# Loading the w3 matrices of the experts through the pool engine's DMA queue

## The chip, the cores and the metric

The kernel runs on one core of one Trainium2 chip, in float32. The metric is device time in microseconds (us). Three runs of the kernel before gave 3997.15 us as their median, from 3993.39 to 4002.57 us.

## The reference

Two transformer blocks run over 512 tokens of width 1024. The first has windowed attention beside retention, then a mixture of 64 experts; the second has two layers of latent attention, pooling and an mLSTM, each followed by a gated feed-forward part. The change touches the mixture of experts alone:

```python
def expert_block(args):
    xb, e = args
    hid = jax.nn.silu(xb @ w1[e]) * (xb @ w3[e])
    return hid @ w2[e]
```

`w1[e]` and `w3[e]` are 1024 x 512, `w2[e]` is 512 x 1024, each 2 MiB (2.10 MB) in float32. Each token is sent to two of 64 experts, with a weight for each, and the weighted results are summed.

## The kernel before

The kernel is written in blocks that follow one another; in each, every engine has its own list of instructions, and the lists meet only in semaphores. `moe_block` runs every expert with room for 32 token slots (`CAP`), so it loads all 64 experts' weights: 192 matrices, 403 MB. Experts that get more than 32 tokens would be run again in a further loop (`ov_...`).

The loop has 16 turns (`NIT`), each of two pairs (`pr`), each of two experts (`e2`). There are six weight buffers of 2 MiB: 0 and 2 hold w1 of the pair's experts, 1 and 3 hold w3, 4 and 5 hold w2. No buffer is double, so a matrix of the next pair can be loaded only when TensorE has done with the one before it.

- SyncE (SP) does the loading. For each pair it waits on `up_done` (L1120), issues w1 and w3 of both experts (L1123, L1124: w1, w3, w1, w3), waits on `down_done` (L1126) and issues both w2 (L1129). All go into one queue, in this order.
- TensorE (PE) waits until all four up matrices of the pair are there (L1162), runs 64 matmuls with them (L1169) and raises `up_done`. ScalarE and VectorE form silu times gate (L1238, L1290), TensorE turns the result (L1175), waits for the two w2 and multiplies with them (L1185), and raises `down_done`. After the second pair of a turn it gathers the next 128 token slots (L1151).
- VectorE copies the pair's result out of PSUM (L1294), and ScalarE stores it with a DMA of 256 KB in a queue of its own (L1243).
- GpSimd (POOL) has no work in this block. In the block before, it fills a part of `y_slots` with zeros by one DMA of 4 MiB (L982: 2048 rows of 2 KB). In the block after, it gathers the results by 16 indirect DMAs, each of 128 rows of 2 KB (L1324).

A row of w1 or w3 is 2 KB, of w2 4 KB; `up_src` and `down_src` put row k\*128+p on partition p, so that rows next to each other in a partition do not touch in memory.

Of the kernel before, what the change touches and what calls it, by code (L numbers as in the profile page):

```python
# [1094 lines left out]
def moe_block(nc, m, G, banks, A, y_slots):  # L1095
    w1, w3, w2 = A["moe_w1"][0], A["moe_w3"][0], A["moe_w2"][0]
    NIT = NE // 4
# [3 lines left out]
    def up_dst(slot):  # L1101
        return m.w[slot].rearrange("p (k n) -> p k n", k=KT)

    def down_dst(slot):
        return m.w[slot].rearrange("p (k n) -> p k n", k=FF // P)

    def up_src(w, e):
        return w[bass.ds(e, 1), :, :].rearrange("a (k p) n -> p (a k) n", p=P)

    def down_src(e):  # L1110
        return w2[bass.ds(e, 1), :, :].rearrange("a (k p) n -> p (a k) n", p=P)

    with nc.Block() as block:

        @block.sync
        def _(sp):
            with sp.Fori(0, NIT) as i:
                for pr in range(2):

                    sp.wait_ge(G["up_done"], 2 * i + pr + 1)  # L1120
                    for e2 in range(2):
                        e = 4 * i + 2 * pr + e2
                        sp.dma_start(up_dst(2 * e2), up_src(w1, e)).then_inc(G[f"e_in{2 * e2}"], 16)  # L1123
                        sp.dma_start(up_dst(2 * e2 + 1), up_src(w3, e)).then_inc(G[f"e_in{2 * e2 + 1}"], 16)  # L1124

                    sp.wait_ge(G["down_done"], 2 * i + pr + 1)  # L1126
                    for e2 in range(2):
                        e = 4 * i + 2 * pr + e2
                        sp.dma_start(down_dst(4 + e2), down_src(e)).then_inc(G[f"e_in{4 + e2}"], 16)  # L1129

            n = sp.value_load(m.misc_i[0:1, 1:2], min_val=0, max_val=MORE - 1)
            with sp.If(n > 0):
                sp.wait_ge(G["up_done"], 2 * NIT + 1)
                sp.wait_ge(G["down_done"], 2 * NIT + 1)
                with sp.Fori(0, n) as j:
                    e = sp.value_load(m.eb_i[0:1, bass.ds(j, 1)], min_val=0, max_val=NE - 1)
                    sp.wait_ge(G["ov_down"], j + 1)
                    sp.dma_start(up_dst(0), up_src(w1, e)).then_inc(G["ov_in"], 16)
                    sp.dma_start(up_dst(1), up_src(w3, e)).then_inc(G["ov_in"], 16)
                    sp.dma_start(down_dst(4), down_src(e)).then_inc(G["ov_in"], 16)  # L1140

        @block.tensor
        def _(pe):
# [1008 lines left out]
def program(nc, A, outs, stop=None, start=0):  # L2152
    ctx = ExitStack()
    with ctx:
# [19 lines left out]
        if start <= 1:  # L2174
            own = take(nc, G, ROUTER_SEMS + MOE_SEMS + COMB_SEMS)
            m = moe_memory(arena)
            norm_views(m, m.norm_at)
            if start == 1:
                load_x(nc, m, G, A)
            eb_dram = nc.dram_tensor("further_experts", (1, MORE), i32, kind="Internal").ap()  # L2180
            y_slots = nc.dram_tensor("y_slots", ((MAIN + MORE) * 2 * CAP, 512), f32, kind="Internal").ap()
            norm_block(nc, m, G, banks, 1 - start, "rms", m.hn, A["norm_moe_w"][0])
            router_block(nc, m, G, banks, A, eb_dram, y_slots)
            moe_block(nc, m, G, banks, A, y_slots)
            combine_block(nc, m, G, banks, y_slots)
            if stop == "moe":
                return dbg(nc, G, outs, m.h)
            give_back(nc, G, own)
# [132 lines left out]
```

## Time and profile before

| | |
|---|---|
| median of three runs | 3997.15 us |
| profiled execution, span from its first to its last instruction | 4010.2 us |
| TensorE busy | 3094.7 us (77%) |
| DMA over the span | 587 MB, mean 146 GB/s |
| loads of the experts' matrices | 192 of 2048 KB, median 19.3 us from issue to landing |

The trace gives the profiled execution no time of its own beside its span. It is one execution, and lies 13 us (0.3%) above the median of the runs. The page cuts the span into 40 slices of 100 us; a digit is a busy share in tenths. A line of a group tells the busy time, the mean of one instruction, the engine's idle time just ahead of it and what ended that.

### The profile page before, as it was taken

The page shows a single profiled execution, that of the slowest core. Times are in us where ns is not written, and L with a number is a line of the kernel's source. Part 1 is how long each engine was busy: PE and PEld are TensorE (multiplying, and loading weights), DVE is VectorE, ACT ScalarE, POOL GpSimd, SP SyncE. Part 2 cuts the span into 40 slices and gives each one's busy share as a digit, 9 for nine tenths or more (in the row PEclk, how much of TensorE's full clock was granted, in tenths as well). Part 3 has the DMA queues.
Part 4 walks back from the last instruction along what each step waited for, and adds up shares of the span by engine and source line. Part 5 has one row for each costly group of instructions (what it writes and reads, how often), then busy time and mean ns, then how long its engine had stood idle before and what let it go on. Part 6 is the DMA issues. An engine that isn't in the chain of part 4 may idle for free. (4 is left out here: it accounts for less than half of the span.)

```text
span 4010.2 us, 30222 instructions
## 1 busy us (share of the span) xinstructions
PE 3094.7 (77%) x12308; PEld 1620.9 (40%) x12308; DVE 684.3 (17%) x1670; ACT 492.8 (12%) x969; POOL 271.5 (7%) x302
## 2 busy tenths in 40 slices
PE   7999999998344545545454288879999798799997
PEld 4666666546311212112121154434444454344443
DVE  1222222101300000000000212321110223221202
ACT  1222232110100000000000112200000112010000
POOL 1000013200000000000000210010000100100001
PEclk9999999999577778777777688789999897899998
DMA  4111111121399999999999431012211210212211
GB/s 140 48 48 32 48 37 48 57 80 53 116 348 363 366 354 357 354 363 370 357 353 360 167 97 43 21 53 84 79 68 53 86 44 22 73 49 77 84 64 41
DMA packets 332165, 587.02 MB, mean 146 GB/s; under 512 B 16802, under 2 KB 143010, under 8 KB 331810
## 3 DMA queue, kind: packets, MB, share of 16 engines
q1 hardware_dynamic: 325138, 568.88, 40.0%
q0 software_dynamic: 2320, 8.39, 0.6%
q10 hardware_dynamic: 4608, 8.39, 0.5%
q8 instruction: 67, 1.10, 0.1%
q14 instruction: 32, 0.26, 0.0%
HBM read 570.96 MB, written 14.68 MB: 146 GB/s over the span
## 5 line engine op out<-in xcount | busy, mean ns | idle before, releaser
L1169 PE MATMUL bank<-arena 128*32 128x512 f32 x2048 | 297.8, 746 | 508.9 <-DMA arena<-in_moe_w 508.9
L2081 PE MATMUL bank<-arena 128*128 128x512 f32 x1408 | 608.9, 595 | 1.9 <-PEq L688 1.9
L328 PE MATMUL bank<-arena 128*128 128x384 f32 x1280 | 432.0, 490 | 14.5 <-DMA arena<-in_w_in 14.5
L2081 PEld LDWEIGHTS bank<-arena 128*128 128x128 f32 x1408 | 269.0, 191 | 340.9 <-issue 340.9
L1169 PEld LDWEIGHTS bank<-arena 128*32 128x32 f32 x2048 | 81.8, 134 | 713.4 <-issue 713.4
L328 PEld LDWEIGHTS bank<-arena 128*128 128x128 f32 x1280 | 237.9, 191 | 176.0 <-DMA arena<-in_w_in 14.8
L2093 PE MATMUL bank<-arena 128*128 128x512 f32 x704 | 302.5, 592 | 0.0
L1583 PE MATMUL bank<-arena 128*128 128x512 f32 (+3 forms) x736 | 251.0, 503 | 15.1 <-DMA arena<-in_w_in 15.1
L2093 PEld LDWEIGHTS bank<-arena 128*128 128x128 f32 x704 | 133.8, 190 | 168.4 <-issue 168.4
L1583 PEld LDWEIGHTS bank<-arena 128*128 128x128 f32 x736 | 140.9, 193 | 121.5 <-issue 74.6
L772 PE MATMUL bank<-arena 128*128 128x128 f32 x256 | 56.9, 404 | 167.4 <-POOL arena L731 105.4
L1290 DVE TENSOR_TENSOR arena<-bank,arena 64x512 f32<-64x512 f32 x32 | 22.2, 695 | 781.9 <-ACT arena L1238 781.9
L1185 PE MATMUL bank<-arena 128*32 128x512 f32 x1024 | 140.0, 696 | 15.5 <-ACT arena L1240 14.7
L1151 PE MATMUL bank<-arena 128*128 128x128 f32 x1088 | 127.4, 278 | 25.3 <-DVE arena L1280 25.3
L1151 PEld LDWEIGHTS bank<-arena 128*128 128x128 f32 x1088 | 124.2, 193 | 38.9 <-DVE arena L1280 25.5
L1238 ACT ACTIVATE arena<-bank 64x512 f32<-64x512 f32 x32 | 18.9, 590 | 851.9 <-PE bank L1169 851.9
L772 PEld LDWEIGHTS bank<-arena 128*128 128x128 f32 x256 | 48.0, 214 | 177.8 <-POOL arena L731 114.9
L2036 PE MATMUL bank<-arena 128*128 128x512 f32 x256 | 116.2, 618 | 1.8 <-PEq L1538 1.8
L325 PE MATMUL bank<-arena 128*128 128x512 f32 x256 | 110.9, 593 | 0.0
L2132 DVE TENSOR_SCALAR arena<-arena 128x512 f32<-128x512 f32 x44 | 24.0, 546 | 494.3 <-ACT arena L2108 494.3
L707 ACT ACTIVATE arena<-bank 128x512 f32<-128x512 f32 x64 | 37.4, 597 | 557.0 <-PE bank L772 557.0
L1324 POOL DMA_INDIRECT arena<-y_slots,arena x16 | 17.6, 1099 | 1226.9 <-PEq L1318 1222.4
(291 smaller groups left out, 2724.3 us busy)
## 6 DMA issues: line engine op xcount, KB each, us to landing
arena<-in_moe_w SPq DMA_DIRECT2D x192, 2048.0 KB, 19.3
arena<-in_w_up SPq DMA_DIRECT2D x44, 1024.0 KB, 7.1
arena<-in_w_in SPq DMA_DIRECT2D x52, 512.0 KB, 5.6
arena<-in_w_down SPq DMA_DIRECT2D x10, 2048.0 KB, 7.7
arena<-in_w_in SPq DMA_DIRECT2D x12, 1024.0 KB, 5.2
y_slots<-arena ACTq DMA_DIRECT2D x32, 256.0 KB, 6.5
arena<-in_w_in SPq DMA_DIRECT2D x4, 2048.0 KB, 11.3
arena<-in_w_out SPq DMA_DIRECT2D x4, 2048.0 KB, 7.8
```

What stands on the lines that cost most here:

```text
L325: ins = pe.matmul(banks[s % 2][:, :], w[:, k, tile(b)], m.aT[:, k, :], start=(k == 0), stop=(k == KT - 1))
L328: ins = pe.matmul(banks[s % 2][:, 0:CW], m.aT[:, k, tile(t)], w[:, k, :], start=(k == 0), stop=(k == KT - 1))
L707: act.activation(m.aT[:, 4 * (i % 2):4 * (i % 2) + 4, tile(i // 2)], banks[i % 4][:, :].rearrange("p (a c) -> p a c", a=4), ACT.Copy)\
L772: ins = pe.transpose(banks[i % 4][:, tile(j)], dst[:, t, tile(4 * (i % 2) + j)], m.ident)
L1151: ins = pe.matmul(banks[5 + d // 4][:, tile(d % 4)], m.hn[:, t, tile(d)], m.G[:, t, :], start=(t == 0), stop=(t == T - 1))
L1169: ins = pe.matmul(banks[pr][q:q + CAP, :], m.xt[:, k, c:c + CAP], up_dst(2 * e2 + up)[:, k, :], start=(k == 0), stop=(k == KT - 1))
L1185: ins = pe.matmul(banks[3 + pr][q:q + CAP, :], m.ht[:, f, CAP * e2:CAP * e2 + CAP], down_dst(4 + e2)[:, f, 512 * half:512 * half + 512], s ...
L1583: ins = pe.matmul(out, a, b, start=(i == 0), stop=(i == len(terms) - 1))
L2036: ins = pe.matmul(banks[n][:, :], m.mixT[:, k, tile(t)], slot_view(m, half)[:, k, :], start=(k == 0), stop=(k == KT - 1))
L2081: ins = pe.matmul(banks[2 * (j % 2) + half][:, :], w[:, k, c0:c0 + P], m.aT[:, k, :], start=(k == 0), stop=(k == KT - 1))
L2093: ins = pe.matmul(banks[2 * t + half][:, :], m.hidT[:, k, tile(t)], v[:, k % 4, 512 * half:512 * half + 512], start=(k == 0), stop=(k == N ...
L2132: own.do(dve.tensor_scalar(gc, gp[:, 0:S], m.wf[:, j, 0:1], m.wf[:, j, 3:4], ALU.mult, ALU.add))
```

## The change

SyncE no longer issues the two w3 loads of a pair. GpSimd gets a loop of its own over the same pairs: it waits on the same `up_done` and issues the two w3 loads into its own queue. Buffers, semaphores, the waits of TensorE and the further loop `ov_...` stay.

```diff
@@ moe_block, block.sync
                     for e2 in range(2):
                         e = 4 * i + 2 * pr + e2
                         sp.dma_start(up_dst(2 * e2), up_src(w1, e)).then_inc(G[f"e_in{2 * e2}"], 16)
-                        sp.dma_start(up_dst(2 * e2 + 1), up_src(w3, e)).then_inc(G[f"e_in{2 * e2 + 1}"], 16)
@@ moe_block, after block.sync
+        @block.gpsimd
+        def _(pool):
+            with pool.Fori(0, NIT) as i:
+                for pr in range(2):
+
+                    pool.wait_ge(G["up_done"], 2 * i + pr + 1)
+                    for e2 in range(2):
+                        e = 4 * i + 2 * pr + e2
+                        pool.dma_start(up_dst(2 * e2 + 1), up_src(w3, e)).then_inc(G[f"e_in{2 * e2 + 1}"], 16)
```

## Rows read from the trace of the kernel before

**Rows 1.** The page, sections 1 and 2: the span, DMA busy share in 40 slices.

```profile
span 4010.2 us, 30222 instructions
...
DMA  4111111121399999999999431012211210212211
```

**Rows 2.** The page, section 5, the costliest group: busy, mean ns, idle before.

```profile
L1169 PE MATMUL bank<-arena 128*32 128x512 f32 x2048 | 297.8, 746 | 508.9 <-DMA arena<-in_moe_w 508.9
```

**Rows 3.** Waits from 1100 to 2100 us: us in total, times, longest.

```profile
PE bank L1169 <- DMA arena<-in_moe_w: 446.4, 28, 20.5
...
PE bank L1185 <- DMA arena<-in_moe_w: 0.7, 1, 0.7
```

**Rows 4.** Windows, the expert loop: length; engines' busy us; PEclk, DMA share, GB/s.

```profile
1083.00:2240.00 1157.00, 583.79 (x4279) 252.63 (x4280) 81.02 (x131) 71.47 (x113) 0.00 (x0) 0.75 0.96 355
```

**Rows 5.** Timeline of one pair: start us, us, engine, line.

```profile
1407.28 0.37 SPq L1123 DMA_DIRECT2D arena<-in_moe_w  x1
...
1408.47 3.94 SPq L1123 DMA_DIRECT2D arena<-in_moe_w  x1
...
1409.64 5.34 PE L1185 MATMUL bank<-arena 128*32 128x512 f32 x32 [0.47 <-ACT arena L1240]
...
1412.51 6.38 SPq L1124 DMA_DIRECT2D arena<-in_moe_w  x1
...
1418.98 7.71 SPq L1129 DMA_DIRECT2D arena<-in_moe_w  x2
...
1433.34 8.88 PE L1169 MATMUL bank<-arena 128*32 128x512 f32 x64 [18.36 <-DMA arena<-in_moe_w]
...
1442.29 0.59 ACT L1238 ACTIVATE arena<-bank 64x512 f32<-64x512 f32 x1 [32.70 <-PE bank L1169]
1442.43 0.37 SPq L1123 DMA_DIRECT2D arena<-in_moe_w  x1
```

**Rows 6.** Windows, the moment after w2 has landed and before the next loads flow.

```profile
1443.00:1444.00 1.00, 0.34 (x3) 0.34 (x4) 0.60 (x1) 0.00 (x0) 0.00 (x0) 1.00 0.58 45
```

**Rows 7.** Windows, first and second 12 us of the up loads, two pairs.

```profile
1409.00:1421.00 12.00, 5.50 (x34) 1.26 (x32) 0.69 (x1) 0.39 (x1) 0.00 (x0) 0.81 1.01 349
1421.00:1433.00 12.00, 0.00 (x0) 0.00 (x0) 0.00 (x0) 0.00 (x0) 0.00 (x0) 0.50 1.05 392
...
1480.00:1492.00 12.00, 5.97 (x36) 1.58 (x36) 0.88 (x2) 0.39 (x1) 0.00 (x0) 0.84 0.98 340
1492.00:1504.00 12.00, 0.00 (x0) 0.00 (x0) 0.00 (x0) 0.00 (x0) 0.00 (x0) 0.50 1.05 394
```

**Rows 8.** Windows, the last 8 us of a pair's loads (w2).

```profile
1434.00:1442.00 8.00, 8.00 (x64) 2.23 (x56) 0.00 (x0) 0.00 (x0) 0.00 (x0) 0.81 1.02 409
```

**Rows 9.** DMA queues, 1410 to 1420 us: packets, MB, share of 16 engines' time.

```profile
q1 hardware_dynamic: 1718, 3.48, 101.3%
```

**Rows 10.** DMA queues, 1434 to 1441 us.

```profile
q1 hardware_dynamic: 713, 2.85, 102.0%
```

**Rows 11.** Line L1123, 1080 to 2200 us: issue to landing.

```profile
L1123 SPq DMA_DIRECT2D arena<-in_moe_w x64: 372/1838/4157, 1084.0 to 2194.5; - x64
...
DMA to landing us min/median/max: 8.4/13.8/20.9
```

**Rows 12.** Timeline and DMA issues: the zero fill, KB, us to landing.

```profile
1020.07 1.43 POOL L982 DMA_DIRECT2D y_slots<-arena  x1 [0.32 <-POOL arena L980]
...
y_slots<-arena POOLq DMA_DIRECT2D x1, 4096.0 KB, 14.7
```

**Rows 13.** DMA queues, 1025 to 1028 us (zero fill beside SP's small loads).

```profile
q0 software_dynamic: 276, 1.13, 91.4%
q1 hardware_dynamic: 247, 0.11, 12.8%
```

**Rows 14.** Windows, the same stretch.

```profile
1025.00:1028.00 3.00, 0.00 (x0) 0.00 (x0) 0.00 (x0) 0.00 (x0) 0.00 (x0) 0.50 1.04 414
```

**Rows 15.** Timeline, the first and the last of 16 gathers of 128 rows.

```profile
2243.85 1.06 POOL L1324 DMA_INDIRECT arena<-y_slots,arena  x1 [1222.35 <-PEq L1318]
...
2264.76 1.24 POOL L1324 DMA_INDIRECT arena<-y_slots,arena  x1 [0.30 <-issue]
```

## The prediction

> **What bounds the kernel now.** I read the page's strip of slices first: for some eleven slices from about 1080 us the DMA digit is 9 [rows 1], and nowhere else. That is the expert loop. The costliest groups say who pays: TensorE's up matmuls (L1169) are busy 297.8 us, but TensorE stood idle 508.9 us before them, all of it for the experts' weights [rows 2]. The waits of 1000 us of the loop say that only the up matrices matter: 446.4 us in 28 waits before L1169, against 0.7 us in one wait before the w2 matmuls, L1185 [rows 3]. The window of the whole loop: 1157 us, DMA share 0.96, 355 GB/s, TensorE busy half the time, VectorE 81 us, GpSimd none [rows 4]. So the loop is bound by bytes: 192 matrices of 2.10 MB are 403 MB, and 32 pairs take 1157 / 32 = 36.2 us each.
>
> The timeline of a pair shows the cycle [rows 5]. SP issues the first w1 at 1407.28. TensorE can begin at 1433.34, 26.06 us later, when all four matrices (8.39 MB) are there, works 8.9 us, and SP issues the next w1 at 1442.43. While TensorE works, w2 (4.19 MB) comes in; it is done about when the up matmuls end, and the DMA is short of work for a moment (45 GB/s in the microsecond from 1443 [rows 6]). The cycle is therefore: the time from `up_done` to the landing of four up matrices, plus 8.9 us. w2 is hidden in the 8.9 us plus the issue time, just so. The time that counts is the landing of the last of w1, w3, w1, w3.
>
> How fast do they come? In the first 12 us of a pair the rate is 349 or 340 GB/s, in the second 12 us 392 or 394 [rows 7]; three other pairs that I looked at in the same way had 334 to 341, then 388 or 389. The w2 loads reach 409 [rows 8]. Two causes can be read. First, packets: in the up phase 1718 packets carry 3.48 MB, about 2 KB each [rows 9]; with w2 713 carry 2.85 MB, about 4 KB each [rows 10]. Second, the slow 12 us end about when SP has got rid of the fourth load: its issues from 1407 to 1419 take 0.37, 3.94 and 6.38 us, and SP is full of them until 1418.9 [rows 5]. That looks like a queue that is fed hardly faster than it drains, until the feeder has got ahead; no row proves it.
>
> **The change, part by part.**
>
> *Moved: 64 issues of w3 from SP to POOL (2 for each of 32 pairs).* SP's own time does not bound: it goes from four to two long issues, about 11.6 us of issuing shrinks to about 1 us, and then it waits on `down_done`, which comes at about 1415.0 (L1185 ends [rows 5]) instead of being passed at 1418.9. So w2 is asked for 4 us earlier, but it stands in SP's queue behind both w1. It costs nothing as long as w1 is the last of the four to land; that is the point on which everything turns. POOL has nothing else in the loop [rows 4], so nothing is queued behind its waits but its own next pair, and its gathers come after the block's end.
>
> *Who goes first?* The only stretch where POOL's queue and SP's queue both had work is the zero fill. From 1025 to 1028 us there were 276 packets of POOL's queue (4 KB each: 1.13 MB) beside 247 of SP's [rows 13]: about one for one, whatever their size. If w3 also travels in 4 KB packets (its rows are 2 KB, as those of the zero fill), POOL's queue gets two thirds of the bytes against w1's 2 KB packets. At 395 GB/s that is 263 GB/s: 4.19 MB of w3 take 15.9 us. With the late start below, w3 is in after some 18 us, and w1 after some 21.5 to 22. w1 is last, w2 behind it in the same queue, as now.
>
> *The late start.* Before data can land the zero fill needed 14.7 us [rows 12], of which 4.19 MB at 412 GB/s are 10.2: 4.5 us for starting and finishing. SP's quickest w1 took 8.4 us [rows 11], of which 2.10 MB at 349 are 6.0: 2.4 us. So w3 starts about 2 us later than w1. w1 fills these 2 us, so with w3 ahead in share it costs nothing.
>
> *What is gained.* (a) Packets. 4.19 MB of w3 at 390 GB/s take 10.75 us, at the 409 of 4 KB packets [rows 8] 10.25: 0.5 us a pair. (b) The slow first half. 12 us at the mean of 340 hold 4.09 MB, which at 390 would take 10.5: 1.5 us a pair. If a queue fed by one issuer is the cause, it goes: SP's queue would have to feed only a third of the rate, and in the one stretch where two queues run side by side there is no such loss, 414 GB/s [rows 14]. If the cause is another (sixteen engines starting in step, say), it stays. Bounds: 0 and 1.5 us; it could also be worse than now by as much as it is now, 1.5 us more, if two feeders disturb each other. I take 1.2 us, because the nearest row, of two queues, shows no loss, and leave 0.3 for the 2 us in which w1 runs alone. Sum: 0.5 + 1.2 = 1.7 us a pair, x 32 = 54 us.
>
> *Nothing else changes the cycle.* w2 moves up with w1's end, still 10.3 us for 4.19 MB beside 8.9 us of matmuls. TensorE, VectorE and ScalarE do the same work. ScalarE's store keeps its queue and has two pairs' time.
>
> Of the profiled execution 4010.2 - 54 = 3956 us is left. It stood 13 us above the median of the runs, so the time of runs comes to 3997 - 54 = **3943 us**.
>
> **Two rules of the Trainium skill, which disagree.** "DMA: Bandwidth & Descriptors", section "Issuing engines are not separate DMA queues", says that DMAs of all issuers interleave on the same 16 engines and that more issuers save only issuing time. "Perfetto Trace Analysis", section "DMA Optimizations", says that spreading may help where making descriptors is the bottleneck, shown by an issuer that is full of DMA slices. The rows show both signs: DMA share 0.96, and SP full for 11.6 us of a pair. By the first rule the gain is rival B's; by the second it is part (b) above.
>
> **The rivals.**
>
> *B. The transfer is bound anyway, and nothing moves.* The 16 engines are busy 0.96 of the loop [rows 4], and the bytes stay. For it: in the slow halves the share is already 0.98 to 1.01 [rows 7], so the engines were not idle, only slow, which might be memory. Against: 409 GB/s of w2 show that the share does not tell the rate. It would give 3997 us; with part (a) alone, 0.5 x 32 = 16 us less, 3981.
>
> *C. Slower: w3 lands last.* The place is the landing of the last w3 (L1162's wait). POOL writes its transfers in software; if it needs longer for a pair's 2048 rows than the load phase has, w1 lands early, w2 goes past it, and the DMA later runs dry under the up matmuls. The point at which it decides: 26.06 us from issue to TensorE's start [rows 5], less the 4.5 us of start and finish, leaves 21.6 us, or 10.5 ns a row. Two rows bracket POOL's pace. The zero fill: 2048 rows in at most 10.2 us, 5.0 ns a row [rows 12]. The gathers: 128 rows each, 15 intervals from 2243.85 to 2264.76, 1.39 us each, 10.9 ns a row [rows 15]; a pair would take 22.3 us, plus 4.5 is 26.8, 0.8 us more than now, x 32 = 26 us slower. If VectorE's work holds POOL up (81 us in the loop, 2.5 us a pair [rows 4]) it is 3.3 us, x 32 = 105 us slower. Middle: 3997 + 65 = 4062 us. For it: a software queue that also has to share, 32 times in a row, where the zero fill was one. Against: w3's loads are plain ones like the zero fill, and its data flowed at 414 GB/s. Equal shares of bytes instead of two thirds are a mild form: w3 then starts 2 us late, and finishes up to 2 us late against the even case; with the gain of 1.7 us that comes out near 0.
>
> The Trainium skill, "SBUF — State Buffer", section "DVE blocks DMA" trap, says that descriptors written by GpSimd are held up while VectorE runs in its two-port mode, as an fp32 SBUF copy does. The copies here read PSUM, and the longest VectorE instruction of the loop is under 1 us; no run here shows such a wait yet, and what it would cost at most is the 2.5 us a pair in C.
>
> *D. Faster than I forecast:* everything runs at the 412 GB/s of the zero fill: 8.39 MB in 20.4 us, against 12.3 + 10.7 = 23.0 now: 2.6 us x 32 = 83 us, 3914 us.
>
> **How the numbers follow.** The forecast, w3 first and the slow half mostly gone (3925 to 3970): 0.48. B: 0.17, of which half is no change and half the 16 us of the packets. C: 0.27, from 4005 to 4110, a tail beyond. D: 0.08. A gain or loss of under 0.2% (8 us) is about what a measurement of this kernel can't tell from no change. Faster: 0.48 + 0.08 + 0.07 = 0.63; within 0.2%: the rest of B and of the mild C, 0.10; slower: 0.27. The range leaves out the lower half of D and the upper half of C: 3905 to 4045 us. The likeliest case's own range is 3925 to 3970.
>
> **What would show it.** In the profile after: POOL's queue with 403 / 3 = 134 MB in packets of 4 KB (about 33,000), SP's with 268 MB. The first 12 us of a pair at 385 GB/s or more. The wait before L1169 ended by w1, not by w3; w3's landings around 18 us after issue, w1's second around 22. SP's second w1 issued at once. Idle before L1169 down from 508.9 us to about 455. If instead w3 lands last, w2 lands while TensorE still works and the DMA share falls, it is C. If POOL's packets are 2 KB, part (a) is wrong, and the share of bytes with it.

## The result and the profile after

The changed kernel takes 4011.65 us (median of 13 runs), the kernel before 3997.06 (median of 13 on the same chips). The ratio is 1.003, 95% interval 1.0016 to 1.0045: slower by 0.3%, some 12 us, where 54 us less were forecast.

The page of the changed kernel: span, queues, the up matmuls, POOL's issues, landings. The queue q1 is SP's, q0 is POOL's, and q10, further below, is ScalarE's; for each stand its packets, its MB and its share of the 16 engines' time.

```profile
span 4007.8 us, 30353 instructions
...
q1 hardware_dynamic: 258578, 434.66, 30.9%
q0 software_dynamic: 36112, 142.61, 9.7%
...
L1178 PE MATMUL bank<-arena 128*32 128x512 f32 x2048 | 293.7, 737 | 524.3 <-DMA arena<-in_moe_w 524.3
...
L1149 POOL DMA_DIRECT2D arena<-in_moe_w x64 | 56.4, 885 | 1123.5 <-PE bank L1178 1060.0
...
arena<-in_moe_w SPq DMA_DIRECT2D x128, 2048.0 KB, 25.4
arena<-in_moe_w POOLq DMA_DIRECT2D x64, 2048.0 KB, 20.3
```

TensorE's idle time before the up matmuls is 524.3 us against 508.9 [rows 2], 15.4 more; up and w2 matmuls together are busy some 9 us less, which leaves about 6 us. From the first load's issue to the last up matmul, too, it is 1150.1 us against 1143.7, 6.4 more. That is what the trace shows of the 12; its span is one execution, and lies below the median of its kernel's runs as the one of before lay above.

A pair in the timeline of the changed kernel, to be read beside [rows 5]:

```profile
1409.58 1.00 SPq L1123 DMA_DIRECT2D arena<-in_moe_w  x2
1410.06 1.76 POOL L1149 DMA_DIRECT2D arena<-in_moe_w  x2 [33.72 <-PE bank L1178]
...
1415.65 12.30 SPq L1128 DMA_DIRECT2D arena<-in_moe_w  x2
...
1435.90 9.83 PE L1178 MATMUL bank<-arena 128*32 128x512 f32 x64 [20.31 <-DMA arena<-in_moe_w]
...
1445.94 1.00 SPq L1123 DMA_DIRECT2D arena<-in_moe_w  x2
```

SP issues both w1 in 1.0 us and POOL both w3 in 1.8; the issuing that filled 11.6 us is gone. Yet TensorE starts 26.3 us after SP's first issue, against 26.06.

How fast the loads flow is read in windows of 12 us. Data begins about 1 us after the first issue, so a window that starts a little sooner after the issue shows a lower rate, whatever the kernel. The window at 1409 in [rows 7] starts 1.72 us after its pair's issue, the one at 1480 only 0.99 us after its own (1479.01). Set at 1.72 us as well, the second has 360 GB/s and not 340:

```profile
1480.73:1492.73 12.00, 5.49 (x34) 1.16 (x32) 0.69 (x1) 0.39 (x1) 0.00 (x0) 0.81 1.01 360
```

The changed kernel, in the same pair of the timeline and in the next but one, set at 1.72 us after the issue (the last two columns are DMA share and GB/s):

```profile
1411.30:1423.30 12.00, 3.81 (x34) 0.93 (x32) 0.69 (x1) 0.39 (x1) 0.52 (x1) 0.90 1.00 347
1423.30:1435.30 12.00, 0.00 (x0) 0.00 (x0) 0.00 (x0) 0.00 (x0) 0.00 (x0) 0.50 1.03 389
...
1483.14:1495.14 12.00, 3.81 (x34) 0.93 (x32) 0.69 (x1) 0.39 (x1) 0.52 (x1) 0.90 0.99 354
1495.14:1507.14 12.00, 0.00 (x0) 0.00 (x0) 0.00 (x0) 0.00 (x0) 0.00 (x0) 0.50 1.03 388
```

Over 31 pairs, all set so, the first 12 us have 349 GB/s on average against 353 before, and the 12 us behind 389 against 391. Both halves are a little slower, not faster. The first 12 us in three pieces:

```profile
1411.30:1415.30 4.00, 3.52 (x34) 0.93 (x32) 0.00 (x0) 0.39 (x1) 0.52 (x1) 1.00 0.99 310
1415.30:1419.30 4.00, 0.29 (x4) 0.00 (x0) 0.69 (x1) 0.00 (x0) 0.00 (x0) 1.00 0.98 328
1419.30:1423.30 4.00, 0.00 (x0) 0.00 (x0) 0.00 (x0) 0.00 (x0) 0.00 (x0) 0.71 1.03 404
```

The kernel before has 335, 345 and 367 there (shown at e8). In the first piece POOL's queue has hardly begun. The queues from 1411 to 1415 us:

```profile
q1 hardware_dynamic: 558, 1.14, 89.3%
q0 software_dynamic: 4, 0.02, 2.5%
```

The median over the pairs: w1's first data comes 1.0 us after SP's first issue, w3's 5.2 us after it. The second w3 has landed 24.7 us after the first issue, the second w1 26.3 us. Who waited for w1, in the whole loop (nobody is listed for w3):

```profile
  PE bank L1178: 524.3, 32
```

The queues of the changed kernel from 1424 to 1432 us, both at work:

```profile
q0 software_dynamic: 515, 2.04, 66.4%
q1 hardware_dynamic: 512, 1.05, 36.3%
```

515 packets against 512: one for one, w3 with 4 KB a packet and two thirds of the bytes, as foreseen from [rows 13]. Together they make 3.09 MB in 8 us, 386 GB/s.

### The profile page after: what moved, and what is told of

The parts are those of the page before. It is cut to its first block and busy times, and to the rows that moved or that the text cites. A ratio compares the mean times of both kernels' runs of the same rounds, so it can differ in the third digit from the quotient of the medians.

```text
span 4007.8 us, 30353 instructions
## 1 busy us (share of the span) xinstructions
PE 3076.1 (77%) x12308; PEld 1613.4 (40%) x12308; DVE 684.4 (17%) x1670; ACT 494.4 (12%) x969; POOL 328.9 (8%) x366
## 5 line engine op out<-in xcount | busy, mean ns | idle before, releaser
L1178 PE MATMUL bank<-arena 128*32 128x512 f32 x2048 | 293.7, 737 | 524.3 <-DMA arena<-in_moe_w 524.3
L1149 POOL DMA_DIRECT2D arena<-in_moe_w x64 | 56.4, 885 | 1123.5 <-PE bank L1178 1060.0
L1194 PE MATMUL bank<-arena 128*32 128x512 f32 x1024 | 134.9, 673 | 15.8 <-ACT arena L1249 14.8
```

Of the source, the lines that this page charges most:

```text
L1149: pool.dma_start(up_dst(2 * e2 + 1), up_src(w3, e)).then_inc(G[f"e_in{2 * e2 + 1}"], 16)
L1178: ins = pe.matmul(banks[pr][q:q + CAP, :], m.xt[:, k, c:c + CAP], up_dst(2 * e2 + up)[:, k, :], start=(k == 0), stop=(k == KT - 1))
L1194: ins = pe.matmul(banks[3 + pr][q:q + CAP, :], m.ht[:, f, CAP * e2:CAP * e2 + CAP], down_dst(4 + e2)[:, f, 512 * half:512 * half + 512], s ...
```

## The experiments

Each ratio is to the kernel before, with its 95% interval. The edits are shown shortened; dots stand for what is left out. Rates are GB/s of all queues together.

**e1: w3 through ScalarE's queue.**

```diff
-                        sp.dma_start(up_dst(2 * e2 + 1), up_src(w3, e)).then_inc(...)
...
+                    act.wait_ge(G["up_done"], 2 * i + pr + 2)
+                    if not (last and pr):
+                        load_w3(i if pr == 0 else i + 1, 1 - pr)      # act.dma_start, next pair
```

> w3 goes through ScalarE's hardware queue instead of POOL's: each pair's two w3 loads are issued when the pair before has done its up matmuls, right before silu. Theory 1 (the slow first 12 us of a pair, 340 GB/s against 390, come from a hardware queue that is fed too slowly with 2 KB rows, each queue for itself): two queues feed at once, the slow half goes, 1.5 us a pair, 48 us in all, about 3950 us. Theory 2 (it comes from the memory or from 16 engines that start in step, or from one feeder that all hardware queues share): the time of before, 3997, within 10 us. Theory 3 (what ate the gain is the software queue: its late start and its longer packets beside another queue): better than the changed kernel by its 14 us, so 3997 or less. Packets should be 2 KB in both queues, one for one, so that w1 and w3 land together.

4021.46 us, ratio 1.0067 (1.0046 to 1.0088). It is no better than the changed kernel as a whole, so theory 3 did not come true. But two things are in that time, and they pull apart. The first 12 us of a pair, set at 1.72 us after the issue, are faster: 375 GB/s in the pair issued at 1412.00, 373 on average over 31 pairs, where before has 353 and the changed kernel 349. Here w3's first data comes 2.8 us after the first issue and not 5.2. Against it, from 1434 to 1438 the last of w3 shares with SP's w2:

```profile
q1 hardware_dynamic: 295, 1.04, 66.9%
q10 hardware_dynamic: 287, 0.56, 37.3%
```

One for one again, but now w2 (q1, mostly 4 KB) has the longer packets: 1.04 MB against 0.56. The up matrices are late by what w2 took: on average 1.18 MB of w2 had moved when TensorE began the up matmuls, against 0.55 MB before. That is 1.6 us at 390 GB/s (an estimate), more than the faster start gives back, and TensorE starts 0.6 us later in a pair.

**e2: all six loads through POOL.**

```diff
-        sp loop: w1, w3, w1, w3; wait down_done; w2, w2
+        the same loop on block.gpsimd, pool.dma_start for all six
```

> All six loads of a pair go through POOL's queue, in the order of before (w1, w3, w1, w3, then w2 after down_done); SP loads nothing in the loop. All packets should be 4 KB and run alone. Theory 1 (slow feeding of the hardware queue): no slow half, 8.39 MB at 409 GB/s are 20.5 us against 23.0, less 2.0 us for POOL's later start: 0.5 us a pair better, 3981 us. Theory 2 (memory or start in step): the slow half stays, 1.5 us, so 1.0 us a pair worse, about 4029 us. If POOL's pace of writing rows bounds (10.9 ns a row, as in the gathers, would be 22.3 us for the up matrices alone and 28 us with w2's rows), the rate of the loop falls to some 290 GB/s and the time rises by over 150 us.

4031.51 us, ratio 1.0102 (1.0061 to 1.0144), as theory 2 had it (4029). The slow first part is there without any hardware queue. Data begins 1.6 us after POOL's issue here; in windows that start 0.6 us after the first data, as those of before do, the first 12 us have 367 GB/s in the pair issued at 1413.35 and 362 on average over 31 pairs (351 before, set in the same way), and the 12 us behind 388. It also settles the packets. The queues of e2 from 1428 to 1436 (w1 and w3 in POOL's packets), and of the kernel before from 1434 to 1442 (w2):

```profile
q0 software_dynamic: 777, 3.10, 102.5%
```

```profile
q1 hardware_dynamic: 815, 3.27, 102.2%
```

Both are packets of 4 KB, but 777 against 815 in the same time, 388 GB/s against 409. POOL's packet holds two 2 KB rows that do not touch in memory, w2's one row of 4 KB. It is not POOL's queue that is slower: e2's own w2, in the same queue, has the 409 too.

```profile
1440.00:1448.00 8.00, 8.00 (x56) 2.19 (x52) 0.00 (x0) 0.00 (x0) 0.00 (x0) 0.72 1.02 409
```

**e3: 16 KB in one piece.**

```diff
-        return w[bass.ds(e, 1), :, :].rearrange("a (k p) n -> p (a k) n", p=P)
+        return w[bass.ds(e, 1), :, :].rearrange("a (p k) n -> p (a k) n", p=P)
-                        ins = pe.matmul(banks[5 + d // 4][:, tile(d % 4)], m.hn[:, t, tile(d)],
+                        ins = pe.matmul(banks[5 + d // 4][:, tile(d % 4)], hn_cols(t, d),   # columns d, d+8, ...
...   (in the same way for w2 and for the turning of hid: columns f, f+4, ...)
```

> The kernel before with another order of rows: partition p gets rows 8p to 8p+7 of w1 and w3 (4p to 4p+3 of w2), so that each partition reads 16 KB in one piece; the gather and the turning of the hidden values take every 8th (4th) column to match. The same bytes, queue and order. Theory 1 (too many rows per byte for the feeder): the slow half goes and all run at 409 GB/s or more: 2.5 us a pair, 80 us, about 3917 us. Theory 2 (memory or start in step): only the packet size helps, 1.0 us a pair, 32 us, about 3965 us. If neither packets nor rows matter: 3997 us.

3904.69 us, ratio 0.9791 (0.9750 to 0.9833). Some 85 to 90 us less for the same bytes, in the same queue and order: theory 1's time. Both parts of it are in that gain, the faster flow of long pieces and the slow start, which hardly exists here (see e8); so it does not tell the two apart.

**e4: w2 through POOL, w1 and w3 on SP.**

```diff
-                    sp.wait_ge(G["down_done"], ...); sp.dma_start(down_dst(4 + e2), down_src(e))
+                    pool.wait_ge(G["down_done"], ...); pool.dma_start(down_dst(4 + e2), down_src(e))
```

> The other split: w1 and w3 stay on SP, the two w2 loads go through POOL's queue after down_done. This tests that queues take turns packet by packet. w2 is then no longer behind the up matrices: it starts some 11 us after the up loads, when about 4.2 to 4.4 MB of them are left, and takes two thirds of the bytes (4 KB packets against 2 KB) for 16 us. The up matrices land about 10 us later, all of it exposed, and then the DMA has nothing to do under the 8.9 us of up matmuls: about +9 to +10 us a pair, +290 to +340 us, 4290 to 4340 us, DMA share of the loop near 0.75. If a queue that came first kept its precedence: 3997 us.

4330.86 us, ratio 1.0843 (1.0794 to 1.0891), inside what was expected. A pair of e4:

```profile
1406.65 0.37 SPq L1123 DMA_DIRECT2D arena<-in_moe_w  x1
...
1413.34 1.47 POOL L1145 DMA_DIRECT2D arena<-in_moe_w  x2 [42.16 <-PE bank L1190]
...
1443.24 7.34 PE L1174 MATMUL bank<-arena 128*32 128x512 f32 x37 [30.58 <-DMA arena<-in_moe_w]
```

TensorE starts 36.6 us after the first issue, 10.5 later than before: all of w2 went past the up matrices. Which queue a load stands in decides who waits, and it is worth over 330 us here.

**e5: the changed kernel with 16 KB in one piece.** The edit is e3's on the changed kernel.

> The changed kernel (w3 through POOL's queue) with 16 KB in one piece for each partition, as in e3. Theory 1 (a second queue costs something of its own: POOL starts 2 to 4 us late, and two streams of packets disturb each other): the changed kernel's 14 us are there again beside e3 (3905), about 3919. Theory 2 (what cost was the many 2 KB rows that POOL writes): no difference from e3, 3905, or a gain. If turns are taken packet by packet and packets are 16 KB in one queue and 4 KB in the other, w3 (4 KB) gets a fifth of the bytes, lands after w1 and w2, and the time rises by 8 us a pair, about 4160.

3988.50 us, ratio 0.9983 (0.9960 to 1.0007): 84 us above e3, far more than theory 1 had, and not by the mechanism of its last sentence, since POOL's packets are 16 KB too. A pair, and the DMA at its end:

```profile
1402.07 0.86 SPq L1129 DMA_DIRECT2D arena<-in_moe_w  x2
1402.55 1.12 POOL L1155 DMA_DIRECT2D arena<-in_moe_w  x2 [33.60 <-PE bank L1184]
...
1408.23 0.81 SPq L1134 DMA_DIRECT2D arena<-in_moe_w  x2
...
1428.13 8.66 PE L1184 MATMUL bank<-arena 128*32 128x512 f32 x64 [19.96 <-DMA arena<-in_moe_w]
```

```profile
1433.00:1438.00 5.00, 3.78 (x36) 0.94 (x28) 0.53 (x1) 0.59 (x1) 0.53 (x1) 1.00 0.21 72
```

With equal packets the queues share the bytes about evenly (1.33 and 1.15 MB from 1420 to 1426 us). w3's first data comes 4.6 us after the first issue, w1's 1.0, so w1 is through first, w2 shares with the last of w3 (TensorE waited for w3 in all 32 pairs), TensorE starts 26.06 us after issue, as in the slow layout, and then the DMA is dry (72 GB/s for 5 us). This is rival C of the prediction, brought about by the packets' size.

**e7: the second expert's w1 and w3 held back.**

```diff
                         e = 4 * i + 2 * pr + e2
+                        if e2:
+                            sp.wait_ge(G["e_in0"], 32 * i + 16 * pr + 16)
```

> The kernel before, but SP issues the second expert's w1 and w3 only when the first expert's w1 has landed, some 8 us after its issue, with one matrix still in the queue. It tells apart why a pair's first 12 us are slow (340 GB/s). Theory 1 (SP's feeder makes rows of 2 KB hardly faster than they drain, so that it is slow while it makes rows): all four matrices are now made while others drain, the slow stretch grows from 12 to over 20 us, about +1 to +1.5 us a pair, 4030 to 4045 us. Theory 1b (the third and fourth load, pressed into a full queue, disturb the first two): the first 8 us run at 390, the time falls by up to 1 us a pair, about 3965 us. Theory 2 (the start from an empty queue, the engines in step): the same 12 slow us, 3997 us within 10.

3999.09 us, ratio 1.0017 (0.9999 to 1.0034): theory 2. SP's first two issues take 0.9 us together, the other two follow 8.7 us later, and the slow stretch is where it was: 356 GB/s from 1403.7 to 1415.7 us, 389 in the 12 us behind, in a pair whose loads were issued at 1401.98 (356 and 391 over 31 pairs). SP full of issues was a companion of the slow stretch and not its cause.

**e8: e3 with the columns of hn copied into order once.**

```diff
+            for t in range(T):
+                dve.tensor_copy(m.hn2[:, t, :].rearrange("p (k q) -> p k q", k=KT),
+                                m.hn[:, t, :].rearrange("p (q k) -> p k q", k=KT))
```

> e3, with the columns of hn put once into the order that the gather needs (4 copies on VectorE ahead of the loop, hidden under the first loads), so that the gather reads them in one piece. In e3 the gather took 15.5 us instead of 7.4, and in every second pair TensorE got to the up matmuls by it and not by the loads. If that is all: up matrices at 430 GB/s in 19.5 us plus 2.4 to start and land plus 8.9 of matmuls, 31 us a pair against 32.5: about 45 us less than e3, 3860 us. If the strided read cost nothing that mattered: 3905.

3908.45 us, ratio 0.9780 (0.9742 to 0.9817): as e3, not 45 us less. The gather is back at 7.4 us from 15.5 and nobody waits for it, but the pair ends no sooner: in the pair from 1414.58 TensorE starts the next up matmuls 23.35 us after the issue. I had reckoned 430 GB/s from the first byte, 22 us. Another part of the missing gain is in the up matmuls themselves (busy time, mean ns of one), of e3 and of e8:

```profile
L1175 PE MATMUL bank<-arena 128*32 128x512 f32 x2048 | 276.7, 700 | 304.2 <-DMA arena<-in_moe_w 298.3
```

```profile
L1176 PE MATMUL bank<-arena 128*32 128x512 f32 x2048 | 298.1, 746 | 418.0 <-DMA arena<-in_moe_w 418.0
```

In e3 the long gather keeps TensorE busy until the up matmuls of every second pair begin, and they run wholly at the upper clock level (granted 1.00, 2.4 GHz): 7.09 us from 1435.29. In e8 TensorE has stood idle for 9.9 us before them, they begin at the lower level (0.50, 1.2 GHz) and take 9.59 us, at a mean of 0.73. Over the loop that is 21.4 us, against 0.3 us a pair by which TensorE begins the up matmuls sooner after the last ones (23.6 against 23.9 on average).

e8 also shows what a start on an empty queue is with 16 KB pieces. The first 12 us of the pair issued at 1447.73, from 1.72 us after the issue, and the same of the kernel before, in its pair of [rows 5]:

```profile
1449.45:1453.45 4.00, 3.52 (x35) 1.00 (x33) 0.00 (x0) 0.39 (x1) 0.00 (x0) 1.00 0.87 373
1453.45:1457.45 4.00, 0.38 (x4) 0.00 (x0) 0.69 (x1) 0.00 (x0) 0.00 (x0) 0.91 0.97 414
1457.45:1461.45 4.00, 0.00 (x0) 0.00 (x0) 0.00 (x0) 0.00 (x0) 0.00 (x0) 0.50 1.02 431
```

```profile
1409.00:1413.00 4.00, 3.53 (x18) 0.82 (x20) 0.00 (x0) 0.39 (x1) 0.00 (x0) 0.59 0.98 335
1413.00:1417.00 4.00, 1.98 (x20) 0.44 (x12) 0.69 (x1) 0.00 (x0) 0.00 (x0) 0.98 1.02 345
1417.00:1421.00 4.00, 0.00 (x0) 0.00 (x0) 0.00 (x0) 0.00 (x0) 0.00 (x0) 0.87 1.02 367
```

With 16 KB pieces the flow is near its full rate in the second piece; with 2 KB pieces it is below it for all three. So an empty queue alone does not make the slow 12 us; short pieces belong to it.

**e9: e8, the up loads in halves.**

```diff
-                    sp.wait_ge(G["up_done"], 2 * i + pr + 1)
+                    for h, sem in enumerate(("up_half", "up_done")):      # up_half: raised after k 3
+                        sp.wait_ge(G[sem], 2 * i + pr + 1)
+                        ks = slice(4 * h, 4 * h + 4)
...
+                                sp.dma_start(up_dst(j)[:, ks, :], up_src(w, e)[:, ks, :])
```

> e8, with each up load cut in two halves (k 0 to 3, k 4 to 7; 1 MB each, 8 KB in one piece): the first halves of the next pair are issued when TensorE has done k 3 of this one, half way through its 8.9 us. If the cycle is bound as I read it (landing of the up matrices plus 8.9 us, with the DMA empty for 1 to 2 us at the turn), the DMA no longer runs dry: 12.8 MB a pair at 425 GB/s, 30.2 us, about 25 to 35 us less than e8, 3830 us. If the DMA was never short of work: the time of e8.

3833.57 us, ratio 0.9591 (0.9554 to 0.9628). This is the version that beats both kernels, by 163 us against before. Its loop:

```profile
1083.00:2065.00 982.00, 552.32 (x4140) 249.96 (x4144) 83.59 (x133) 69.93 (x110) 0.00 (x0) 0.80 1.00 416
```

416 GB/s over the loop, against 355 [rows 4].

**e10: the kernel before, in halves only.** The edit is e9's alone; rows stay 2 KB, all on SP.

> The kernel before with the cut in halves of e9 alone (rows stay 2 KB, all on SP): the next pair's first halves are in the queue before this pair's up matmuls end. Theory 2 (a pair's slow first 9 to 12 us come from starting on an empty queue): the DMA is never empty, so the dry moment (0.9 us a pair) and the slow start (up to 1.5 us) both go, 3920 to 3970 us, and the rate of the loop is level. If the slow stretch belongs to the up matrices' rows wherever they begin: only 0.9 us a pair, about 3970 us, and the dips stay.

3912.32 us, ratio 0.9773 (0.9744 to 0.9803): the whole of theory 2's gain (3920 us at best) and 8 us more. The whole loop, and two stretches of 12 us in it:

```profile
1083.00:2140.00 1057.00, 555.33 (x4216) 248.46 (x4220) 80.30 (x130) 70.98 (x112) 0.00 (x0) 0.78 1.02 389
1413.00:1425.00 12.00, 9.90 (x89) 6.57 (x82) 1.56 (x3) 1.58 (x3) 0.00 (x0) 1.00 1.04 387
1425.00:1437.00 12.00, 2.51 (x26) 2.35 (x28) 1.99 (x3) 1.88 (x2) 0.00 (x0) 0.82 1.04 393
```

The loop runs at 389 GB/s. Up matrices that begin behind w2, without an empty queue between, have no slow first part.

**e11: e10 with w3 through POOL.** The change under test, on top of e10.

```diff
+        pool loop: wait up_half, first halves of both w3; wait up_done, second halves
```

> e10 with w3 through POOL's queue, in the same halves: the change under test, made where no load starts from an empty queue and POOL's late start lies behind w2's last bytes. Theory: what the change costs is the second start (w1 alone for some 4 us, then w3 starts and is slow again); then it costs nothing here, e11 equals e10 within 8 us. But POOL's first halves can now go past w2 of the running pair, since queues take turns: w2 may land late and hold the down matmuls up, which costs nothing as long as the up matrices come later still. If a POOL transfer costs more per byte: e11 is 14 us or more above e10.

3911.02 us, ratio 0.9759 (0.9725 to 0.9793): as e10. Its loop:

```profile
1083.00:2140.00 1057.00, 562.15 (x4202) 249.06 (x4205) 80.50 (x130) 70.98 (x112) 95.62 (x128) 0.78 1.02 389
```

The same 389 GB/s. So POOL's queue costs nothing per byte, and gains nothing.

**e12: e1 with one w2 on ScalarE's queue.**

```diff
-                        sp.dma_start(down_dst(4 + e2), down_src(e)).then_inc(G[f"e_in{4 + e2}"], 16)
+                    sp.dma_start(down_dst(4), down_src(4 * i + 2 * pr)).then_inc(G["e_in4"], 16)
+                    # slot 5: act.dma_start for the next pair, behind the store of y
```

> e1 (w3 on ScalarE's queue) with one of the two w2 on ScalarE's queue too, so that both queues hold w1/w3 first and a w2 behind. In e1 the first 12 us of a pair moved 4.29 MB against 4.04 before, yet the up matrices landed later, 26.7 us after issue against 26.1. Theory (w1 is through first, SP's w2 in 4 KB packets then takes two thirds from the last of w3): with w2 split evenly this lateness shrinks, and e12 is better than e1's 4021 by 15 to 40 us, near or under 3997. If e1 was slow for what ScalarE has to issue: 4021 or more.

4025.79 us, ratio 1.0053 (1.0036 to 1.0070), not to be told from e1. The expected 15 to 40 us did not come, and the trace shows why: w2 still goes past w3 by as much, 1.16 MB on average before TensorE's start against 1.18 in e1, and TensorE waited for ScalarE's w3 in 30 pairs, as in e1. ScalarE's queue is the later one in both. That w2 costs e1 its time rests on these amounts; no run took w2's share away.

**e13: pieces of 4 KB for w1 and w3.**

```diff
+        return w[bass.ds(e, 1), :, :].rearrange("a (q p j) n -> p (a q) (j n)", p=P, j=2)
```

> The kernel before with w1 and w3 read in pieces of 4 KB (two rows that touch, 4 pieces for each partition) in place of 2 KB; w2 as before, the gather helped by the copies of e8. I had put w2's 409 GB/s down to the packets of 4 KB; e2, where POOL made 4 KB packets of two 2 KB rows, took 173 ns a packet against 164 for w2's, so it is the piece that touches in memory. If so: up matrices at 409 too, 1.0 us a pair better, 3965 us; and if the slow start belongs to 2 KB pieces, it goes as well, 3917. e8 with 16 KB gave 3908.

3954.33 us, ratio 0.9866 (0.9835 to 0.9897), between the two expectations. SP makes these packets as before; with the longer piece the later part of a pair runs at 414 GB/s (1439 to 1450 us). Its first 12 us, set at 1.72 us after the issue, have 388 and 380 in two pairs:

```profile
1392.92:1404.92 12.00, 3.81 (x34) 0.94 (x32) 0.69 (x1) 0.39 (x1) 0.00 (x0) 0.81 1.02 388
1427.00:1439.00 12.00, 11.53 (x89) 7.32 (x88) 0.87 (x2) 0.99 (x2) 0.00 (x0) 0.86 0.98 380
```

Over 31 pairs it is 391 and then 413, 5% apart, where before has 353 and 391, 10% apart: the slow start shrinks by about half but does not go. A part of the gain is lost in the up matmuls, which are busy 309.3 us in all against 297.8.

## Why the prediction was wrong

The forecast was 54 us less, the sum of two terms, (a) 0.5 and (b) 1.2 us a pair. Both came out at nothing, and the late start, priced at nothing, cost a little.

- **What bounds the loop, and the cycle: right.** e9 and e10 took the DMA's dry moment and slow start away and the loop fell by about what they were worth. The cycle was right in shape; that it restarts from an empty queue 32 times was in [rows 6], and the prediction put no price on it.
- **Who goes first: right in kind.** One packet for one, w3 with two thirds of the bytes, w1 last in all 32 pairs, w2 behind it. The times were too short: w3 was to be in after 18 us and w1 after 22, and they landed after 24.7 and 26.3. The sum for w1 had left out the start and the slow half. e4 and e5 show what happens where the order does not hold.
- **The late start costs nothing: wrong, by a small amount.** The step took w3 to start 2 us after w1; it starts 4.2 us after it. The 2 us came from the zero fill, which was one DMA. POOL's queue is not always so late: in e2, where it is alone, data comes 1.6 us after the issue, and beside SP's queue 4.8 us after it. With w1 nearly alone the first 4 us run at 310 GB/s against 335. On average over the pairs TensorE starts 0.3 us later after the up matmuls' end (26.75 against 26.44), 10 us in 32 pairs; 0.1 us of it is in the first 12 us (349 against 353 GB/s), the rest in the 12 us behind (389 against 391) and in w2, of which 0.61 MB went past against 0.55. It fits the loss, but no run took POOL's late start away by itself.
- **Part (a), packets, 0.5 us a pair: wrong.** The step put w2's 409 GB/s down to packets of 4 KB. e2 has 4 KB packets of w1 and w3 at 388 GB/s, the rate of 2 KB rows, and w2 in the same queue at 409; e13 has 414 with 4 KB pieces. The term is 0: what counts is the piece that touches in memory.
- **Part (b), the slow half, 1.2 us a pair: wrong, and this failed the forecast.** Its base was too large: 1.5 us a pair came from 340 GB/s, a figure of windows that partly start before the flow; the 353 of all pairs against 391 make 1.2 us. The step then read SP's long issues [rows 5] as a queue fed too slowly, and took as its nearest row a stretch of the zero fill that begins 5 us after the fill's issue, past its start, and goes to memory, not from it. e7 moved the issues and left the slow part in place, and e10 took it away with one queue and the same rows. It needs a start on an empty queue (e10) and short pieces (e8, e13), and the change keeps both. A second queue can win back a part: e1, where the second queue's data is 1.8 us behind the first's, has 373 GB/s where before has 353, half of the loss. The changed kernel has two queues as well and wins nothing; that this is for w3's start 4.2 us behind w1's fits these rows and is not shown. Why the engines are slow after such a start no run shows.
- **Rival B, "nothing moves", is nearest in its mechanism**, with 0.17. The Trainium skill's first rule, that issuers share the same engines and only issuing time is saved ("DMA: Bandwidth & Descriptors", section "Issuing engines are not separate DMA queues"), agrees with e10 and e11, 389 GB/s each; after a start on an empty queue e1 does not quite fit it. Its other rule, balance where an issuer is full ("Perfetto Trace Analysis", section "DMA Optimizations", of the Trainium skill), looked at a sign (SP full) that e7 shows to be no bottleneck here.
- **Rival C has the nearer number, and did not happen.** The measured time lies at the lower end of its 4005 to 4110 us, but w3 never landed last. Its cause is not there: POOL was not slow in writing rows, its two w3 issues took 1.76 us. Its form, a later queue whose up matrices are passed by w2, is real in e5.

## What to carry to other kernels

Before crediting a second DMA queue with a gain, look at what the transfers do after the queue ran empty and what size of piece touches in memory. Here not running empty was worth 90 us (e10), longer pieces 85 to 90 (e3), both together 163 (e9), the second queue nothing (e11). Moving loads to another queue also takes away the order that one queue gave; packets take turns one for one, so work out from packet sizes and start times which load lands last, and what goes past it. An issuer that is full of DMA instructions may only be waiting for room: spread its issues, as e7 did, before taking it for the bottleneck. And when the rates of two kernels are compared in windows, set the windows at the same distance from the issue, and over many pairs: 0.7 us of shift made 340 of 360 GB/s here, more than the change itself did.

## What the runs showed of the hardware

- A load phase of 2 KB rows that starts on an empty queue ran at 353 GB/s (343 to 375) in the 12 us from 1.72 us after its issue and at 391 in the 12 us behind, from SP's queue (before; e7 356 and 391); from POOL's queue (e2) at 362 and 388, set from its first data. Behind other loads there was no such part (e10, 387). With 4 KB pieces the first 12 us had 391 against 413 behind (e13), with 16 KB pieces 409 against 431 (e8), and of that most is the first 4 us.
- The rate went with the piece that is contiguous in memory: 387 to 394 GB/s for 2 KB, 409 to 414 for 4 KB (w2, e13); with 16 KB and halves the whole loop had 416 (e9).
- POOL's queue made packets of 4 KB from two separate 2 KB rows, and packets of 16 KB where pieces were 16 KB: in e5 from 1420 to 1426 us the two queues had 81 and 86 packets with 1.33 and 1.15 MB.
- The queue that joins another starts late. Issued within half a microsecond of SP's loads, POOL's data came 4.8 us after POOL's issue (changed kernel; 4.1 in e5) and ScalarE's 2.8 us after its own (e1), SP's 1.0 us after; POOL's queue alone needed 1.6 us (e2).
